# A three-block transformer kernel: block 1's input norm is moved from its rows to the results of its matmuls

## The reference

```
def rms_norm(x, g):
    y = xf * lax.rsqrt(jnp.mean(xf * xf, axis=-1, keepdims=True) + RMS_EPS)
    return (y * g.astype(jnp.float32)).astype(x.dtype)

h = rms_norm(x, norm_mix_g[l])
(f_q, f_k, f_v, f_f, n_q, k_c, v_c, k_s, v_s, k_w, v_w, n_g, g_a, g_b) = split_cols(h @ w_in[l])
...                                  # forgetting attention and sparse attention on the first 2848 columns
mix = jax.nn.sigmoid(g_a) * out_a + jax.nn.sigmoid(g_b) * out_b
x = x + mix @ w_out[l]
x = x + hierarchical_moe(rms_norm(x, norm_ffn_g[l]), ...)   # 16 experts
return second_block(x, ...)          # two more layers, with their own norms
```

## Time and profile before

| | |
|---|---|
| Median of 3 runs | 983.77 us (983.37 to 989.74) |
| The profiled execution | 983.33 us, span 981.5 us |
| PE busy | 960.9 us, 98% of the span |
| DVE, ACT, POOL busy | 817.3, 673.2, 51.4 us |
| HBM read | 208.72 MB |

### The profile page before, as it was taken

The page is one execution under the profiler, slowest core; times in us unless marked ns, Lnnn a source line. Parts: engine busy times, 40 slices in busy tenths (PEclk is TensorE's granted clock), DMA queues, the critical chain, the costliest instruction groups (busy, mean ns, idle before and its releaser), DMA issues.

```text
span 981.5 us, 18320 instructions
## 1 busy us (share of the span) xinstructions
PE 960.9 (98%) x7041; PEld 819.8 (84%) x7041; DVE 817.3 (83%) x1608; ACT 673.2 (69%) x1358; POOL 51.4 (5%) x48
## 2 busy tenths in 40 slices
PE   7999999999999999999999999999999999999997
PEld 6878989977888888888878999887887999988786
DVE  5999868868999999999988878798578977697684
ACT  6476676557889889898875577856456477765652
POOL 1202000001001020020000000000001000000010
PEclk9999999999999999999999999999999999999999
DMA  8643272444999999999954543344453444333421
GB/s 348 224 172 120 104 291 103 166 171 187 387 372 355 408 371 343 401 361 377 388 209 152 194 148 130 128 144 162 151 214 136 179 145 164 130 128 133 172 86 43
DMA packets 32232, 210.98 MB, mean 215 GB/s; under 512 B 3600, under 2 KB 3600, under 8 KB 9360
## 3 DMA queue, kind: packets, MB, share of 16 engines
q1 hardware_dynamic: 30560, 204.22, 55.1%
q10 hardware_dynamic: 1584, 5.56, 1.6%
HBM read 208.72 MB, written 1.05 MB: 214 GB/s over the span
## 4 chain that ended last, share of the span: by engine, by line
PE 84%; DVE 8%; ACT 5%; issue 2%; POOL 1%; DMA 0%; DVEq 0%; POOLq 0%; ACTq 0%
PE ps L614 24%; PE ps L616 23%; PE ps L615 23%; PE ps L619 4%; DVE w_lo L463 2%; PE ps L781 2%; PE ps L811 2%; PE ps L1120 1%; ACT w_hi L2089 1%; ACT s_buf L2133 1%; ACT buf_c L2089 1%; POOL stat L475 1%; DVE s_buf L1403 1%; DMA head<-in_head 0%; DVE scr L463 0%
## 5 line engine op out<-in xcount | busy, mean ns | idle before, releaser
L463 DVE TENSOR_TENSOR w_lo<-ring,w_hi 128x512 fp32r<-128x512 f32 (+1 forms) x624 | 393.0, 681 | 63.7 <-ACT w_hi L2089 62.4
L2089 ACT ACTIVATE w_hi<-ring 128x512 fp32r<-128x512 f32 (+1 forms) x624 | 355.3, 623 | 92.8 <-PE ps L616 88.4
L614 PE MATMUL ps<-w_hi,op_rows 128*128 128x512 f32 (+2 forms) x784 | 306.7, 391 | 9.8 <-ACT zin L2505 2.8
L616 PE MATMUL ps<-w_hi,op_rows 128*128 128x512 f32 (+2 forms) x784 | 301.0, 384 | 0.0
L615 PE MATMUL ps<-w_lo,op_rows 128*128 128x512 f32 (+2 forms) x784 | 300.6, 383 | 0.0
L614 PEld LDWEIGHTS ps<-w_hi,op_rows 128*128 128x128 f32 x784 | 147.3, 188 | 42.4 <-DVE w_lo L463 7.7
L616 PEld LDWEIGHTS ps<-w_hi,op_rows 128*128 128x128 f32 x784 | 147.3, 188 | 29.6
L615 PEld LDWEIGHTS ps<-w_lo,op_rows 128*128 128x128 f32 x784 | 147.5, 188 | 27.6 <-issue 0.5
L614 PE MATMUL ps<-op_rows,w_hi 128*128 128x256 f32 x544 | 158.4, 291 | 0.0
L615 PE MATMUL ps<-op_rows,w_hi 128*128 128x256 f32 x544 | 153.7, 283 | 0.0
L616 PE MATMUL ps<-op_rows,w_lo 128*128 128x256 f32 x544 | 153.7, 283 | 0.0
(11 more groups left out here) (277 smaller groups left out, 1138.5 us busy)
## 6 DMA issues: line engine op xcount, KB each, us to landing
ring<-in_panels SPq DMA_DIRECT2D x161, 1024.0 KB, 5.0
keys<-in_panels SPq DMA_DIRECT2D x16, 1024.0 KB, 7.1
two_ends<-in_panels SPq DMA_DIRECT2D x16, 1024.0 KB, 7.3
cst<-in_c ACTq DMA_DIRECT2D x1, 1229.0 KB, 8.8
ring<-in_panels ACTq DMA_DIRECT2D x2, 512.0 KB, 5.9
buf_a<-in_pre ACTq DMA_DIRECT2D x2, 512.0 KB, 5.9
keys<-in_post ACTq DMA_DIRECT2D x2, 512.0 KB, 3.4
head<-in_head ACTq DMA_DIRECT2D x1, 580.0 KB, 4.4
```

The costliest lines, as they stand in the source:

```text
L463: return V.tensor_tensor(o, a, b, op)
L614: T.matmul(o, l[0], r[0], start=start, stop=False)
L616: return T.matmul(o, l[1], r[0], start=False, stop=stop)
L2089: return A.activation(o, a, ACT.Copy, scale=scale)
```

## The change

Block 1 multiplies `x * g` without the factor, and the factor comes in where results leave PSUM.

- `norm_scale` is gone. `norm_turns` turns `x_tok` itself and waits only for its load (`ld_x`, `ld_x1`).
- At the head of ACT's and DVE's programs the order is another: the turned rows come before the first pieces of weight, and the squares and sums of a group stand behind pieces and rows (the three order listings below).
- The banks of `z` are copied out by instructions that multiply by the token's factor, a number per partition: ACT by its scale, DVE by a `tensor_scalar`.
- For the gates, whose tokens lie along the row, the factor must be a row in every partition. Behind take 4 DVE writes two 128x128 diagonals of the factor times -2 (`factor_diagonal`, into `rs_rows`), PE multiplies them by a matrix of -1/2 (`factor_rows`, one fp32 matmul of 128x256 into bank 7), and behind take 6 DVE copies the bank back to `rs_rows` (`factor_out`). The gate banks are then read by DVE with a `tensor_tensor` multiply (eight of 128x512) in place of ACT's copy.
- The 62 last loads (from number `PARTED` = 132 on, those of the two last layers) are each issued as two DMAs of 512 KB, the first when the first two pieces of the slot are split, the second when the last two are. The second parts count on the semaphores of slots 4 and 5.

```diff
@@ -48,6 +48,7 @@
 WIDE, NARROW = N_FIRST + RING, N_FIRST + 6 * N_EXP
+PARTED = NARROW + RING
 
...
@@ -179,7 +180,7 @@
 def beside_block1():
-    table = {3: [("lower", 0)], 5: [("fox_sums", 0)], 7: [("fox_norms", 0)], 9: [("fox_sums", 1), ("fox_q", 0)],
+    table = {3: [("lower", 0)], 4: [("factor_diagonal", 0), ("factor_rows", 0)], 5: [("fox_sums", 0)], 6: [("factor_out", 0)], 7: [("fox_norms", 0)], 9: [("fox_sums", 1), ("fox_q", 0)],
              11: [("forget", 0), ("fox_norms", 1)], 12: [("log_in", 0), ("nsa_gates", 0)], 13: [("fox_k", 0)],
...
...
@@ -428,6 +431,13 @@
             ahead_of[load], last[s] = last.get(s), load
+        tails, tail_of = {}, {}
+        for s in (4, 5):
+            tails[s] = max(in_slot[load] for load in in_slot if slot_of(load) == s)
+        for load in range(PARTED, len(halves)):
+            s = 4 + load % 2
+            tails[s] += 1
+            tail_of[load] = (s, tails[s])
 
...
@@ -450,6 +460,8 @@
                 return ld_first, 16
+            if load in tail_of and part >= 2:
+                return slot_ld[tail_of[load][0]], 16 * tail_of[load][1]
             return slot_ld[slot_of(load)], 16 * in_slot[load]
...
@@ -580,6 +592,19 @@
                 before, s = ahead_of[load], slot_of(load)
+                if load in tail_of:
+                    for h in range(2):
+                        for p in pieces:
+                            if p.load == before and p.part // 2 == h:
+                                sp.wait_ge(w_lo_done[p.lo], p.lo_count)
+                        c = slice(h * HALF // 2, (h + 1) * HALF // 2)
+                        if h == 0:
+                            sem_ = slot_ld[s]
+                        else:
+                            sem_ = slot_ld[tail_of[load][0]]
+                            sp.wait_ge(sem_, 16 * (tail_of[load][1] - 1))
+                        nc.sync.dma_start(ring[:, s * HALF + c.start:s * HALF + c.stop], panels[index, :, c]).then_inc(sem_, 16)
+                    continue
                 if before is None:
...
@@ -625,9 +650,9 @@
             def norm_turns(a):
+                pe.wait_ge((ld_x, ld_x1)[a], 16)
                 for k in range(KT):
-                    pe.wait_ge(norm_x, 2 * a + k // 4 + 1)
-                    m = turn128(norm_at(a, k), scr[:, a * D + k * P:a * D + (k + 1) * P])
+                    m = turn128(norm_at(a, k), x_tok[:, a * D + k * P:a * D + (k + 1) * P])
                     if k % 2 and (a == 0 or k % 4 == 3):
...
@@ -718,6 +743,11 @@
                 return i
+
+            def factor_rows(_):
+                pe.wait_ge(norm_ms, 3)
+                T.matmul(ps[:, 7, 0:S], minus_half[:, 0:1].to_broadcast([P, P]), rs_rows, start=True,
+                         stop=True).then_inc(rows_mm, 1)
 
...
@@ -1255,11 +1285,15 @@
 
-            def norm_scale(a):
-                dve.wait_ge(norm_rs, a + 1)
-                for c in range(2):
-                    o = slice(a * D + c * 512, a * D + (c + 1) * 512)
-                    ts(scr[:, o], x_tok[:, o], stat[:, 2 + a:3 + a], None, ALU.mult).then_inc(norm_x, 1)
+            def factor_diagonal(_):
+                dve.wait_ge(norm_rs, TT)
+                for a in range(TT):
+                    m = ts(rs_rows[:, a * P:(a + 1) * P], ident, stat[:, 2 + a:3 + a], -2.0, ALU.mult, ALU.mult)
+                m.then_inc(norm_ms, 1)
+
+            def factor_out(_):
+                dve.wait_ge(rows_mm, 1)
+                dv(V.tensor_copy(rs_rows, ps[:, 7, 0:S]))
 
...
@@ -1970,17 +2004,15 @@
 
-            norm_sum(0)
-            norm_scale(0)
-            feed(2)
             norm_los(0, 0)
...
             norm_los(0, 1)
+            feed(6)
+            norm_sum(0)
             feed(8)
-            norm_sum(1)
-            norm_scale(1)
             norm_los(1, 0)
             norm_los(1, 1)
+            norm_sum(1)
             dve.wait_ge(ld_prm, 16)
...
@@ -1989,7 +2021,8 @@
                     dve.wait_ge(taken, t + 1)
-                    V.tensor_copy(z3[:, 1, n * 512:n * 512 + cols], ps[:, 1, 0:cols]).then_inc(out_free[1], 1)
+                    dve.wait_ge(norm_rs, 2)
+                    ts(z3[:, 1, n * 512:n * 512 + cols], ps[:, 1, 0:cols], stat[:, 3:4], None, ALU.mult).then_inc(out_free[1], 1)
                 if t == T_Z + 13:
...
@@ -1999,6 +2032,13 @@
                 ahead(t)
+                b, f = feature_at(T_GATE, t)
+                if f:
+                    c = (4 * ((t - T_GATE) // 4) + 2 * b) * S
+                    settle()
+                    dve.wait_ge(taken, t + 1)
+                    tt(gates[:, c:c + 512].rearrange("p (f t) -> p f t", f=2), ps[:, b, :].rearrange("p (f t) -> p f t", f=2),
+                       rs_rows.unsqueeze(1).to_broadcast([P, 2, S]), ALU.mult).then_inc(out_free[b], 1)
                 behind(t)
...
@@ -2407,15 +2447,15 @@
             ac(A.activation(stat[:, 4:5], minus_half[:, 0:1], ACT.Square))
+            norm_his(0, 0)
+            feed(2)
+            norm_his(0, 1)
+            feed(6)
             norm_square(0)
-            feed(2)
-            norm_his(0, 0)
-            feed(4)
-            norm_his(0, 1)
             feed(8)
-            norm_square(1)
             norm_his(1, 0)
             norm_his(1, 1)
+            norm_square(1)
             act.wait_ge(ld_prm, 16)
...
@@ -2428,17 +2468,12 @@
                     act.wait_ge(tok_mm, i + 1)
-                    copy(z3[:, 0, n * 512:n * 512 + cols], ps[:, 0, 0:cols]).then_inc(out_free[0], 1)
+                    act.wait_ge(norm_rs, 1)
+                    copy(z3[:, 0, n * 512:n * 512 + cols], ps[:, 0, 0:cols], stat[:, 2:3]).then_inc(out_free[0], 1)
                 steps(t, "scores_out")
...
                 ahead(t)
-                n = (t - T_GATE) // 4
-                b, f = feature_at(T_GATE, t)
-                if f:
-                    c = (4 * n + 2 * b) * S
-                    act.wait_ge(taken, t + 1)
-                    copy(gates[:, c:c + 512], ps[:, b, :]).then_inc(out_free[b], 1)
                 behind(t)
...
                 which, i = divmod(t - T_UP, 4)
```

More of the change, by code:

```diff
@@ L305, in build @@
         pick = sb("pick", 8, F32R)[:, :]
-        comb_r = sb("comb_r", 64, F32R)[:, :]
+        at_r = col()
+        rs_rows = sb("rs_rows", S)[:, :]
+        comb_r = sb("comb_r", 64, F32R, at_r)[:, :]
         assert col() <= 53200
@@ L377, in build @@
         dve_step, act_step, pool_step = sem("dve_step"), sem("act_step"), sem("pool_step")
-        norm_sq, norm_ms, norm_rs, norm_x, norm_T, norm_hi, norm_lo = (
+        norm_sq, norm_ms, norm_rs, rows_mm, norm_T, norm_hi, norm_lo = (
             sem("norm_" + n) for n in ("sq", "ms", "rs", "x", "T", "hi", "lo"))
@@ L1160, in hg_turn @@
                     pair_turns(ZI + 2 * b * P, b, zb3).then_inc(back_T, 1)
-            table = {"fox_q": fox_q, "fox_k": fox_k_, "nsa_side": nsa_side, "scores": scores, "turn": turn,
+            table = {"factor_rows": factor_rows, "fox_q": fox_q, "fox_k": fox_k_, "nsa_side": nsa_side, "scores": scores, "turn": turn,
                      "values": values, "compress": compress, "swa_sides": swa_sides, "level": level, "cross": cross,
@@ L1955, in dve_program @@
                      "up_split": up_split, "att_split": att_split, "hg_turn": hg_turn,
-                     "compress": compress, "rope": rope, "swa_sides": swa_sides, "level": level, "head_norm": head_norm,
+                     "compress": compress, "factor_diagonal": factor_diagonal, "factor_out": factor_out, "rope": rope, "swa_sides": swa_sides, "level": level, "head_norm": head_norm,
                      "head_scale": head_scale}
```

## The result

| | before | after |
|---|---|---|
| Median | 983.77 us (983.29 to 989.74, 7 runs) | 992.71 us (991.11 to 993.96, 7 runs) |
| Ratio of after to before | | 1.0079, 95% interval 1.0064 to 1.0093 |
| The profiled execution | 983.33 us, span 981.5 us | 992.71 us, span 990.9 us |

The change makes the kernel 0.8% slower. The forecast was 988.5 us with a range up to 991.3, so the sign was right and the size too small by 4.2 us; the result lies 1.4 us above the range. By the bound of 1% it is still "no change", as forecast.

A forecast was written before the change was run, and what follows sets the result against it. PE was taken as the bound from 19 us on, ACT's and DVE's splitting at the start. Terms 0.7 + 4.0 + 0.5 + 0 + 0.2 + 0, less 0.2, gave 5.2 us on 983.33: 988.5 us, range 986.2 to 991.3.

The forecast's parts named there:

- the first rival: TensorE's clock falls during PE's wait behind take 4, restarting at 1.2 GHz: 1.5 us more, 990.0 us; chance 0.2.
- The stand: Between takes 4 and 5 PE waits for DVE's two diagonals, queued behind `lower` and pieces: 4.0 us, 3.3 to 4.6.
- the matmul: One fp32 matmul of 128x256 on PE behind take 4: +0.5 us, 0.4 to 0.6.
- The start: Up to group 1's first product, at 19.6: the new order gives back the norm's 0.9 us; +0.7 us, 0.3 to 1.0.
- the turns can follow the constant matmuls at 6.9: At the start, turning `x` as loaded removes 0.9 us of waiting; turns had begun at 7.80.
- No gap inside, the longest 1.8 us, brought it down: Argument from the trace before: gaps up to 1.8 us left TensorE's clock up; it fell 4.7 us after the last matmul.
- The banks: Copying out `z` with the factor costs 0, ends -0.2 to +0.3; 0.2 us of bank wait may go.
- the gates: Eight multiplies move to DVE, which has idle time; PE waits at take 38: +0.2 us, 0 to 0.7.
- a DVE-bound gate stage: Rival: the eight gate multiplies land on PE's path with all 5.4 us: 993.9 us; chance 0.05.
- a stand that is paid back: Rival: PE in takes 5 to 23 runs at DVE's pace and recovers the wait: 982.4 to 983.5 us; chance 0.05.
- parted loads: In the last layers, half loads remove a wait that isn't there: 0, ends -0.3 and +0.3 us.
- The clock rival: TensorE drops to half clock during PE's wait behind take 4, 1.5 us more: 990.0 us; chance 0.2.

The follow-up runs named there:

- the wait alone: Kernel before plus the diagonals, the matmul behind take 4 and the copy behind take 6, their result unused: 990.50 us, ratio 1.0056.
- the kernel turned early with parted loads: The second experiment's kernel, with PE turning group 1 between the second and third step of group 0, squares and sums behind group 1's rows: 983.62 us, 0.9993.
- the first experiment: Kernel after with `factor_rows` moved from behind take 4 to behind take 8 and `factor_out` to behind take 10: 986.85 us, ratio 1.0029.
- the second experiment: The first experiment's kernel with the start's order as in the kernel before, pieces 0 and 1 ahead of the first turned rows: 985.47 us, 1.0008.
- six constants: The first experiment's kernel with six constant matmuls instead of nine at the head of PE's queue: 986.78 us, ratio 1.0021.
- the parted kernel: Kernel before with only the last 62 loads parted, run twice: 986.51 us, ratio 1.0021, then 985.00 us, 1.0002.

## Why the prediction was wrong, step by step

**Which step failed.** Chiefly the weighing of the first rival. The prediction said "A stand of 4.0 us lies between these" and gave the fall of the clock 0.2, because the stand "is still short of the only gap that did". That compared the stand with the end of the span, where the clock could be seen to fall 4.7 us after the last matmul. But both ends, the 1.8 us that left the clock up and the 4.7 us that brought it down, were of *one* execution. In all three profiles with the stand (after, the wait alone, after with whole loads; 3.74 to 3.80 us) the clock fell. And the end of the span gives no bound either: over the fourteen profiles the clock falls between 2.0 and 5.3 us after PE's last matmul. In the kernel turned early with parted loads that matmul ends at 975.50, and the clock is down from 977.5 on:

```profile
977.50:979.00 1.50, 0.00 (x0) 0.00 (x0) 1.12 (x2) 0.00 (x0) 0.00 (x0) 0.51 0.10 40
```

The rival's price was of the right size: it gave 1.5 us, and the traces show 1.7, 2.4 and 1.3. The Trainium skill's page "TensorE: Matmul & The Clock Gate" (Part 1, the HAM clock gate), by which an idle TensorE goes back to half clock, agrees with these three traces; the rule that the prediction set against the gaps of one trace was the better guide.

**The stand.** Forecast 4.0 us for the wait and 0.5 for the matmul, measured 3.80 and, with the restart, 4.31 in sum. The wait alone shows it without the rest of the change, and both ways around it (matmul later, diagonals first) take it away, so this cause is shown. With the matmul and the clock behind it, it cost 6.0, 7.0 and 5.9 us in the three profiles that have it, counted from group 1's first product to POOL's first power.

**The start.** Forecast +0.7 us, measured +1.98 in the profiled execution of after. The step "the turns can follow the constant matmuls at 6.9" was the wrong one. It took the constants' 5.67 us of one trace as fixed. They took from 5.62 to 6.88 us over the thirteen profiled executions with nine constants, for they run partly at half speed, and for how long differs: between 5 and 6 us PE takes up four of their rows after and six in the kernel before. (This is read from the rows alone; the clock column of the windows has 1.00 there in all kernels.) Before, the norm's chain hid that: with 5.67 us of constants the turns stood at 7.80, with 5.99 us at 7.61. The change takes the cover away, and after 6.88 us the turns stand at 7.97, 1.07 us later than forecast. From the turns' start on the chain was nearly as worked out: 12.89 us to group 1's first product in the profile of after, 12.7 forecast. In the first experiment with the turns at 6.72, the first product stood at 10.30 (10.25 forecast) and group 1's at 19.74 (19.6), so 0.86 of the start's term is the order's, as the second experiment confirms. That the exposed length costs only in one direction (six constants gave back 0.3 of 1.17 us) fits the third step's wait.

**The second fall**, 1.4 us at 918, was in no term. "No gap inside, the longest 1.8 us, brought it down" was true of one execution only. Executions of the kernel before lie in three heaps, in the last batch 10 from 983.1 to 984.1 us, 10 from 984.9 to 985.7 and 3 from 986.7 to 987.1, some 1.7 us apart, which is the size of one fall (the profiled executions of the kernel before, 983.33 and 983.97 us, are of the first heap and show none). But a fall is not all that makes a heap: executions of it at 984.96, 985.03 and 985.11 us have a mean granted clock of 1.000, and the gap of issue of the parted kernel cost 1.8 us without a fall. The forecast was built on an execution with neither. It is not shown that the change makes this fall likelier.

**What held.** The banks (the wait of 0.2 us for one is no longer in PE's list); the gates (+0.2 forecast, 8.00 to 8.23 us of delay measured, though at the turns of `scr` behind the last multiply and not at take 38's); the rivals of a DVE-bound gate stage and of a stand that is paid back were both wrong, as weighed; parted loads 0, after one set of runs that seemed to say otherwise.

**The sum again**, with what the runs showed: 983.33 + 1.98 + 4.31 + 1.7 = 991.3 without the fall at 918 us, and 992.7 with it. Of the 4.2 us that the forecast lacked, 1.3 are the start's, 1.7 the clock's behind the stand and 1.4 the second fall's, less 0.2 by which stand and matmul came out shorter. The second fall is a matter of the execution; that the median is the one that was profiled, with this fall in it, is chance. The clock rival's 990.0 with the start's true size, 991.3, was the forecast to make. The forecast's upper end of 990.3 leaves out the +0.3 that it gave the banks; with it, it is 990.8, which changes neither the range nor the outcome.

## What to carry to other kernels

When the bound engine gets an instruction that waits for another engine, look at what stands ahead on that engine's queue: here one swap (the diagonals ahead of `lower`) or a later place saved 4.8 to 5.9 us of the change's 8.9. A stand of TensorE costs its length and then the half-clock stretch behind it (1.3 to 2.4 us for one of 3.8); if a stand is longer than any gap known to leave the clock up, take the fall as the likeliest case. And work that a removed step had covered comes to light with all of its spread, so ask what stood beside the removed step, not only how long it was. The gain came only after the order of the start was rebuilt around it, and it is small: POOL's first power 1.4 and 1.6 us earlier than before in the two profiles of that order, 0.16% below the kernel before in one set of runs and 0.07%, with 1 inside the interval, in the other.

## What was not expected of the hardware

- TensorE's clock does not fall at a fixed length of a gap. Over the profiles of all kernels, the two waits between layers when they were whole (1.69 to 1.84 us, behind a run of small matmuls on 32 columns of weights) were followed by half clock in 8 of 21 cases, the wait of 2.55 us at the start in 3 of 5, and the stand of 3.7 to 3.8 us in 3 of 3. Of the waits of 0.2 to 1.05 us at those places none was. In one and the same execution both occur: in the first experiment's profile a wait of 1.82 us ahead of 679.38 was followed by half clock and one of 1.82 us ahead of 913.55 was not. The first of these two rows, of that profile's windows, is behind the former; the second, of the parted kernel's second run, is behind a wait of 1.83 us at the same place.

```profile
681.00:683.00 2.00, 2.00 (x6) 1.60 (x5) 2.00 (x4) 1.98 (x5) 0.00 (x0) 0.50 0.52 176
```

```profile
680.00:682.00 2.00, 2.00 (x11) 1.65 (x10) 2.00 (x5) 2.00 (x5) 0.00 (x0) 1.00 0.32 123
```

- PE has gaps of issue (up to 1.6 us) that no wait explains. Splitting DMAs on SP's queue moved one of them away from PE's stream at 673 us in seven of eight profiles, though PE's program is the same. What they are stays open; they cost nothing there, since the wait 5 us later is shorter by more (1.05 for 1.83 us behind a gap of 0.52). Elsewhere they can cost: behind the one of 1.57 us at 640.71 every row was 1.8 us later. So they are as large as a fall of the clock, and two profiles may differ by one or the other.
- A 95% interval from one batch can leave out 1 by 0.1% for a change that does nothing (1.0021, from 1.0010; again 1.0002). With heaps some 1.7 us apart, the share of executions in each heap is what a median of ten reads.
